# Where the transposes of the decayed keys stand in a two-way gated linear attention: before or after the outputs from the states

## The reference

```python
b = jnp.cumsum(gc, axis=2)
b_last = b[:, :, -1:]
q_dec = qc * jnp.exp(b)
k_intra = kc * jnp.exp(-b)
k_state = kc * jnp.exp(b_last - b)
scores = jnp.where(mask, jnp.einsum('bnthd,bnshd->bnhts', q_dec, k_intra), 0.0)
o_intra = jnp.einsum('bnhts,bnshv->bnthv', scores, vc)
def step(S, xs):
    qd, ks, vv, bl = xs
    o = jnp.einsum('bthd,bhdv->bthv', qd, S)
    S = S * jnp.exp(bl)[..., None] + jnp.einsum('bthd,bthv->bhdv', ks, vv)
    return S, o
```

## Time and profile before

| What | Value |
| --- | --- |
| median of three runs | 1323.81 us |
| profiled execution, its own time | 1320.3 us |
| its span | 1318.1 us |
| PE busy | 1289.7 us (98%) |
| DVE, ACT, POOL busy | 561.5, 686.0, 723.5 us |
| the eight combinations on PE | from 139.53 to 200.82 us of the span |

### The profile page before, as it was taken

The page is one execution under the profiler, slowest core; times in us unless marked ns, Lnnn a source line. Parts: engine busy times, 40 slices in busy tenths (PEclk is TensorE's granted clock), DMA queues, the critical chain, the costliest instruction groups (busy, mean ns, idle before and its releaser), DMA issues.

```text
span 1318.1 us, 21900 instructions
## 1 busy us (share of the span) xinstructions
PE 1289.7 (98%) x8008; PEld 1084.5 (82%) x8008; DVE 561.5 (43%) x1065; ACT 686.0 (52%) x1096; POOL 723.5 (55%) x335
## 2 busy tenths in 40 slices
PE   5999999999999999999999999999999999999999
PEld 1688678787888888888777648999999987999999
DVE  3425572126444433300047454555532584566610
ACT  3562356335444444422257754666664667866642
POOL 0442224352544444454437023688899765888897
PEclk8999999999999999999999999999999999999999
DMA  9532753642223233533534253556666541666664
GB/s 358 181 96 96 264 216 128 247 184 80 96 96 95 95 95 95 223 112 98 208 131 134 64 191 128 199 194 192 191 207 209 174 132 48 209 193 191 196 203 126
DMA packets 60132, 210.16 MB, mean 159 GB/s; under 512 B 6432, under 2 KB 9760, under 8 KB 59936
## 3 DMA queue, kind: packets, MB, share of 16 engines
q1 hardware_dynamic: 59632, 207.52, 47.2%
q10 hardware_dynamic: 432, 1.70, 0.3%
HBM read 208.15 MB, written 1.05 MB: 159 GB/s over the span
## 4 chain that ended last, share of the span: by engine, by line
PE 94%; DVE 2%; ACT 1%; SPq 1%; DMA 1%; issue 1%; POOL 0%; ACTq 0%; DVEq 0%; POOLq 0%
PE ps L355 75%; PE ps L482 2%; PE ps L410 1%; PE ps L392 1%; PE ps L402 1%; PE ps L1558 1%; DMA raw<-wstream 1%; PE ps L1537 1%; PE ps L1153 1%; SPq L317 1%; PE ps L1141 1%; PE ps L1121 1%; PE ps L1540 1%; PE ps L1161 1%; PE ps L1518 1%
## 5 line engine op out<-in xcount | busy, mean ns | idle before, releaser
L344 POOL TENSOR_TENSOR wlo<-raw,whi 128x1024 fp32r<-128x1024 f32 x291 | 695.5, 2407 | 519.6 <-ACT whi L339 519.0
L339 ACT ACTIVATE whi<-raw 128x1024 fp32r<-128x1024 f32 x291 | 306.7, 1056 | 211.9 <-PE ps L355 146.7
L355 PE MATMUL ps<-Hhi_,whi 128*128 128x256 f32 (+1 forms) x1336 | 388.2, 319 | 0.0
L355 PE MATMUL ps<-Hlo_,whi 128*128 128x256 f32 (+1 forms) x1336 | 384.6, 316 | 0.0
L355 PEld LDWEIGHTS ps<-Hhi_,whi 128*128 128x128 f32 x1336 | 250.9, 188 | 22.2 <-issue 4.1
L355 PEld LDWEIGHTS ps<-Hlo_,whi 128*128 128x128 f32 x1336 | 251.0, 188 | 19.4 <-issue 1.4
L355 PE MATMUL ps<-Hhi_,wlo 128*128 128x256 f32 (+1 forms) x1336 | 231.6, 316 | 0.0
L355 PEld LDWEIGHTS ps<-Hhi_,wlo 128*128 128x128 f32 x1336 | 194.4, 188 | 18.1
L355 PE MATMUL ps<-hidhi,whi 128*128 128x256 f32 (+1 forms) x528 | 151.1, 315 | 0.0
L355 PE MATMUL ps<-hidlo,whi 128*128 128x256 f32 (+1 forms) x528 | 150.7, 314 | 0.0
L778 ACT ACTIVATE u<-ps,par 128x256 f32<-128x256 f32 (+1 forms) x132 | 83.9, 635 | 114.6 <-PE ps L355 101.3
(11 more groups left out here) (344 smaller groups left out, 1562.4 us busy)
## 6 DMA issues: line engine op xcount, KB each, us to landing
raw<-wstream SPq DMA_DIRECT2D x367, 512.0 KB, 3.5
Haside_lo<-wstream SPq DMA_DIRECT2D x8, 512.0 KB, 6.1
Haside_hi<-wstream SPq DMA_DIRECT2D x8, 512.0 KB, 9.2
Paside<-wstream SPq DMA_DIRECT2D x4, 512.0 KB, 5.1
XT<-x_t SPq DMA_DIRECT2D x1, 1024.0 KB, 12.0
XT<-ctx_t SPq DMA_DIRECT2D x1, 1024.0 KB, 14.1
memx<-mem_t ACTq DMA_DIRECT2D x1, 1024.0 KB, 5.3
out_t<-XT SPq DMA_DIRECT2D x1, 640.0 KB, 6.2
```

What stands on the lines that cost most here:

```text
L339: nc.scalar.activation(whi[:, n % RING, :], raw[:, r % RAWS, :], ACT.Copy).then_inc(S["hi_ready"], 1)
L344: nc.gpsimd.tensor_tensor(wlo[:, r, :], raw[:, r, :], whi[:, n % RING, :].bitcast(F32), ALU.subtract).then_inc(S["lo_ready"], 1)
L355: mm = nc.tensor.matmul(o, a, b, start=start, stop=stop)
```

## The change

In the loop over `c` in `gla_pe`, the call of `state_turns(c)` moves from behind `between_blocks(c - 1)` to in front of it. All other code, on all other engines, stays as it is.

```diff
@@ -1164,9 +1164,9 @@
             for c in range(2 * GH):
                 h, d = divmod(c, 2)
                 score(c)
+                state_turns(c)
                 if c >= 1:
                     between_blocks(c - 1)
-                state_turns(c)
                 if d == 0:
                     mod_products(pe, 0, {0: 5, 2: 7, 4: 8, 6: 10}[c])
                 else:
```

## The result

The changed kernel took 1324.42 us (median of 20 runs, 1323.73 to 1331.38). The kernel before took 1322.40 us in the same series (median of 20, 1318.76 to 1326.01). The ratio is 1.0028 with a 95% interval of 1.0014 to 1.0041: slower by 1.9 to 5.4 us, 3.7 us by its middle. That is less than 0.5%, the case to which the forecast gave 0.54, and the time lies inside the range of 1321 to 1335 us; against the 1328 us that the prediction named it is 3.6 us too low. The profiled execution took 1323.73 us, its span is 1321.4 us.

The account below looks back on a forecast made before the run. PE bounds the kernel, busy 98% of the span. Seven steps longer by 0.85 us (6.0 us) less 0.4 us given back make +5.6 us; on the profiled 1320.3 that is 1325.9, on the median 1329.4; 1328 us taken, range 1321 to 1335.

Parts of the forecast that it names:

- What bounds the kernel: Whole span: PE busy 98%; its waits from the recurrence on total 6.6 us, longest 1.2, so added PE time counts fully.
- The sample at combination 0: There the transposes already follow the score products; PE idles 0.82 us for POOL's decay, 1.50 us from L1125 to transposes.
- The sum: Recurrence steps 1 to 7: 3.30 us odd, 3.39 even, against 2.44 and 2.54; 6.0 us more, net +5.6.
- the 0.4 us given back at combinations 3 and 5: `between_blocks` there found its last state late, 0.2 us each; starting later, it would find the states ready.
- What else moves: Recurrence: `between_blocks` ends 1.4 us later, delaying DVE's chain; cover left is 1.8 us at c = 1, 0.7 at c = 3.
- The collision at even combinations: DVE's product L1348 takes 1.67 us instead of 0.69 beside POOL's diagonal doubling; moved later, DVE regains 0.98 us.
- POOL held up by DVE: Rival at POOL's decay of the keys: DVE's two-input products delay it, up to 4.8 us more, 1330.7 us; chance 0.07.
- DVE's chain as the bound: Rival in the recurrence: states late at c = 3, 5 and others, 1 to 3 us on top, 1330 us; chance 0.07.
- A delay taken up later: Rival behind the recurrence: a PE wait absorbs the 5.6 us, leaving 1320.3, or 1322 to 1324 us; chance 0.04.
- No effect: Rival in the recurrence: PE passes the waiting transposes and runs `between_blocks` first; chance 0.03, shared with an unseen gain.
- From the profile to the time: Whole kernel: 5.6 us added to profiled 1320.3 gives 1325.9, to median 1323.81 gives 1329.4; 1328 us taken, up 0.42%.
- The choice of 0.54 for no clear difference: Whole time: chance 0.54 within 0.5% (6.6 us), against 0.43 slower and 0.03 faster, with scatter of 2 to 3 us.

Follow-up runs that it names:

- the kernels with odd and even combinations: Two kernels: transposes moved first only at odd, or only at even combinations, elsewhere as before; 1321.75 us (ratio 1.0020) and 1321.24 us (1.0013).
- the kernel with a tile of its own: Changed kernel, but POOL writes the decayed keys into a separate tile without waiting for the score products; 1323.37 us, ratio 1.0024 to before.
- the second product in the order of before: Kernel before, plus a second equal-sized POOL product, into an unread tile, ahead of the decay of the keys; 1325.14 us, ratio 1.0024.
- the one split at combination 0: Kernel before, with half of combination 0's modulation products placed ahead of the transposes, half behind; 1320.23 us, ratio 1.0005.
- one token: Changed kernel, with POOL's decay of the keys cut to four elements a partition, other tokens' keys undecayed; 1321.38 us, ratio 1.0018 to before.

## Why the prediction was right, point by point

**What bounds the kernel.** Right. PE's waits behind the recurrence are the same rows before and after, and the part behind it changed by 0.1 us. Nothing took the delay up. Two profiles of each kernel show this.

**The sample at combination 0.** Right, and it carried the forecast. The distance of 1.50 us and the wait of 0.82 us came back at seven more places.

**The sum.** I put the step at 3.30 and 3.39 us; it is 3.29 and 3.38. I put the recurrence at 66.9 us; it is 66.79. The growth is 5.5 us against 5.6. Of its two parts, the 0.4 us given back at combinations 3 and 5 is there, and the kernels with odd and even combinations show that either of them alone brings it.

**What else moves.** Right to 0.2 us in each number. DVE's product starts 148.40 - 144.84 = 3.56 us behind L1125 (3.7 expected), the states are done at 154.25 - 144.84 = 9.41 (9.5), and the next `between_blocks` starts at 156.17 - 144.84 = 11.33 (11.3). At combination 3 the states are done at 171.21 and PE starts at 171.97: the cover is 0.76 us (0.7 expected). The collision at even combinations went away.

**The rivals.** POOL held up by DVE (the first in the list, which the prediction calls the second where it speaks of the pair of 1.67 and 1.28 us): not here, each L2155 at the keys takes 0.62 us or less. It can happen, though: in the kernel with a tile of its own POOL's product took 1.05 us beside DVE's. DVE's chain as the bound: not here, but shown to be near by the second product in the order of before, and by the tile of its own. A delay taken up later: no. No effect: no.

**From the profile to the time.** This is the weak step. The prediction took 1328 us, between 1325.9 (from the profile) and 1329.4 (from the median of three runs), and the median is 1324.42; the profiled execution, 1323.73, is also 2.2 us under the first of these, and the part ahead of the recurrence was 2.1 us shorter. As for the difference, the measured middle is 3.7 us, and the recurrence alone would make it 5.5; the interval's upper end is 5.4. In the profiles two other terms move the time, by up to 2.5 and by 5.1 us, and both do so between kernels that are the same there. One is the part ahead of the recurrence, which ended between 137.04 and 139.53 us over the profiles. The other is behind it: in three profiles it takes 1122.3 us and in all others 1117.2 to 1117.9. The chain of work that ended last puts nearly all of that, 5.05 us, at one place, the products of the second feed-forward's first half (start, duration, count), here in the changed kernel, and then in the one split at combination 0:

```profile
846.36 129.32 PE ps L355 x1140
```

```profile
840.55 134.37 PE ps L355 x1140
```

The three executions with 134.37 took 1323.07 (split at 0), 1325.01 (twice, order of before) and 1325.69 us (one token). The first and the third are 2.8 and 4.3 us over the medians of their kernels; the second is 0.1 under its own, of whose ten runs six lie between 1325.0 and 1326.4 and four between 1320.0 and 1320.9. The kernel with a tile of its own has two runs at 1317.28 and 1318.38 us, of which the first is the profiled one with 129.32, and ten from 1322.99 to 1325.05, so that its median lies on the upper level. Single runs of the first series fit this. Those of before fall into ten from 1318.76 to 1321.48 us and ten from 1323.33 to 1326.01, those of the changed kernel into fifteen from 1323.73 to 1325.80 and five from 1329.05 to 1331.38. Level against level, the medians differ by 5.15 us (1319.25 and 1324.40) and by 5.20 us (1324.48 and 1329.68); the medians of all runs differ by only 2.0, since more of the changed kernel's runs are on its lower level. Where before showed the lower level alone (25 runs, 1318.32 to 1320.98), the changed kernel was 5.2 us over it. That the mixture of levels lowered the first ratio, and that these levels are the two durations of that stage, is argued from these lists, not shown by an experiment; that the recurrence grew by 5.5 us is shown.

**The choice of 0.54 for no clear difference** rested on 5.6 us being below 6.6, and on the scatter. With 3.7 measured that case came about, and it would have with 5.2 as well. So the case was not luck, but the 3.7 is smaller than what the change costs by the share of runs on each level. The scatter that I had from four numbers was of the right size, but I took it for one spread, where the lists show two levels.

## What to carry to other kernels

Where engines hand work to and fro, the trace often holds one instance of the arrangement that a change wants everywhere: a first or last round of a loop in which the usual neighbour is missing. Read its distances between starts; here they gave the recurrence to 0.1 us (66.9 against 66.79). A wait is worth its length only where nothing independent stands in its place, and work put there as cover must itself be ready at that point. To find what a small change did, cut the span at two instructions that both kernels have, and compare the parts before comparing times.

## What the runs showed of the hardware that I had not expected

The same 1140 matmuls of 128x256 in the second feed-forward ran at two paces, at the same granted clock of 1.00 and without idle time. The windows of 10 us for L355 alone (length, busy time of PE with its count, granted clock, share of the DMA engines, GB/s) of the kernel with even combinations, and then of the one split at 0:

```profile
853.00:863.00 10.00, 10.00 (x91) 1.00 0.61 204
863.00:873.00 10.00, 10.00 (x91) 1.00 0.59 179
```

```profile
850.00:860.00 10.00, 10.00 (x87) 1.00 0.58 185
860.00:870.00 10.00, 10.00 (x87) 1.00 0.55 184
```

Windows count a matmul that runs across their edge too. It is 90 or 91 against 87 or 88 in 10 us, evenly over the stage, which takes 129.32 or 134.37 us (0.113 or 0.118 us a matmul), never anything between in twelve profiles (nine of the first, three of the second). The 1536 products of a later stage took 174.09 us, 0.113 us each, in all twelve. The code of the stage is the same in all of them. The cause stays open: no experiment was made on it, and no kernel was profiled at both paces.

A handover to POOL and back, with a product of four elements a partition between, costs PE 0.41 us of waiting; 0.20 of it is the product's own duration.
